# Cached keys doubled on load and turned inside the attention; counts, key splits, completions and row copies of a hybrid encoder step placed elsewhere

## The reference, cut to what matters

```python
# index scores, the top 256 keys of each query, then attention over these keys
logits = relu(einsum('bqhd,bld->bqhl', qi, ki))          # 8 indexer heads of 64
index  = einsum('bqhl,bqh->bql', logits, wi)
index  = where(admissible, index, -inf)                   # own chunk of 64 and all before
top_val, sel = top_k(index, 256)
s = einsum('bqkgd,bqnkd->bqkgn', qg, gather(k, sel)) * 64 ** -0.5   # 8 heads, 2 key heads
p = softmax(where(valid, s, -inf)); o = einsum('bqkgn,bqnkd->bqkgd', p, gather(v, sel))
```

## Time and profile before

| | us |
|---|---|
| median of 3 runs | 904.68 (904.44 to 906.88) |
| the profiled execution | 904.78 |
| its span | 903.2 |
| TensorE busy | 801.8 |
| VectorE busy | 484.6 |
| ScalarE busy | 335.1 |
| GpSimd busy | 166.5 |

### The profile page before, as it was taken

How to read it: one execution, slowest core, us unless ns; L and a number is a source line. 1 busy time by engine, 2 the same in 40 slices (tenths; PEclk the granted TensorE clock), 3 DMA queues, 4 the chain that set the end, 5 groups by cost and what they waited for, 6 DMA issues and landing times.

```text
span 903.2 us, 12302 instructions
## 1 busy us (share of the span) xinstructions
PE 801.8 (89%) x4185; PEld 673.1 (75%) x4185; DVE 484.6 (54%) x1188; ACT 335.1 (37%) x753; POOL 166.5 (18%) x361
## 2 busy tenths in 40 slices
PE   4788988898989999689489999999998999999984
PEld 3677877777877878578487788888886888888873
DVE  5523576778796877967852433333355433333323
ACT  4535545656566565566462111111125200000010
POOL 0323314040312103010103211111121111101101
PEclk9899969998989989979789999999999999999997
DMA  9322021211202002003425212111456443333331
GB/s 267 137 69 90 24 90 30 84 32 71 82 20 71 8 12 74 25 1 105 135 84 156 88 64 64 64 64 64 145 150 203 136 114 110 114 116 111 109 82 35
DMA packets 36206, 79.00 MB, mean 87 GB/s; under 512 B 7408, under 2 KB 9856, under 8 KB 34880
## 3 DMA queue, kind: packets, MB, share of 16 engines
q1 hardware_dynamic: 29712, 59.07, 21.0%
q0 software_dynamic: 6448, 19.36, 6.7%
HBM read 57.88 MB, written 20.53 MB: 87 GB/s over the span
## 4 chain that ended last, share of the span: by engine, by line
PE 60%; DVE 19%; issue 7%; ACT 6%; DMA 4%; POOL 2%; SPq 0%; DVEq 0%; POOLq 0%; ACTq 0%
PE bank L797 47%; DVE probs L1517 4%; DMA xT<-turned_x 3%; PE bank L912 3%; DVE work L1423 2%; DVE work L1458 1%; DVE top L1456 1%; PE bank L812 1%; PE bank L858 1%; PE bank L859 1%; PE bank L901 1%; DVE idx L1404 1%; PE bank L980 1%; PE bank L981 1%; PE bank L964 1%
## 5 line engine op out<-in xcount | busy, mean ns | idle before, releaser
L797 PE MATMUL bank<-w_hi,xT 128*128 128x512 f32 (+1 forms) x1152 | 378.8, 399 | 15.5 <-DVE xT L1343 6.7
L797 PEld LDWEIGHTS bank<-w_hi,xT 128*128 128x128 f32 x1152 | 221.0, 194 | 66.4 <-DMA xT<-turned_x 7.6
L797 PE MATMUL bank<-w_lo,xT 128*128 128x512 f32 (+1 forms) x576 | 226.9, 394 | 0.0
L797 PEld LDWEIGHTS bank<-w_lo,xT 128*128 128x128 f32 x576 | 112.2, 195 | 19.4
L912 PE MATMUL bank<-v_sb,pT 128*128 128x64 f32 x648 | 93.7, 286 | 11.3 <-ACT pT L1151 10.9
L912 PEld LDWEIGHTS bank<-v_sb,pT 128*128 128x128 f32 x648 | 87.1, 205 | 18.9 <-ACT pT L1151 18.1
L901 PE MATMUL bank<-ident,probs 128*128 128x128 f32 x324 | 56.8, 289 | 18.2 <-ACT probs L1140 18.0
L1404 DVE SCALAR_TENSOR_TENSOR idx<-bank,iw_s,idx 128x384 f32<-128x384 f32 (+5 forms) x93 | 53.7, 611 | 32.4 <-ACT bank L1186 31.5
L1140 ACT ACTIVATE probs<-probs,low 128x128 f32<-128x128 f32 (+8 forms) x68 | 54.7, 805 | 41.3 <-DVE low L1517 41.2
L1151 ACT COPY pT<-bank 128x512 f32<-128x512 f32 (+3 forms) x104 | 49.0, 495 | 42.5 <-PE bank L901 41.4
L901 PEld LDWEIGHTS bank<-ident,probs 128*128 128x128 f32 x324 | 40.9, 152 | 27.7 <-ACT probs L1140 25.6
(11 more groups left out here) (188 smaller groups left out, 1175.9 us busy)
## 6 DMA issues: line engine op xcount, KB each, us to landing
xT<-turned_x SPq DMA_DIRECT2D x34, 512.0 KB, 4.2
stage<-in_w_in SPq DMA_DIRECT2D x40, 256.0 KB, 3.2
turned_x<-xT SPq DMA_DIRECT2D x9, 1024.0 KB, 5.2
xin<-in_x_prompt SPq DMA_DIRECT2D x16, 256.0 KB, 3.9
early<-in_w_in SPq DMA_DIRECT2D x4, 1024.0 KB, 6.5
y_row<-in_x_prompt SPq DMA_DIRECT2D x16, 256.0 KB, 5.3
stage<-in_w_out SPq DMA_DIRECT2D x16, 256.0 KB, 3.2
out<-y_row POOLq DMA_DIRECT2D x16, 256.0 KB, 2.4
```

The lines of the kernel that those rows point to most:

```text
L797: mm = pe.matmul(out, (lo if which == 2 else hi)[:, k, :], (w_lo if which == 1 else w_hi)[slot][:, k, 0:width], start=(i == 0), stop=(i == ...
```

## The change

Six edits, all in the first part:

1. The cached rows are loaded doubled: two transfers write each 64-element piece side by side twice, so that one transpose fills both halves of the partitions, and one instruction of 128 partitions copies or splits a bank. The indexer keys take two staging buffers and two banks (ci 0 and 1), the keys two loads of xin and four banks (ck 0 for key head 0, ck 1 for key head 1, two banks each). Each has twice the transposes.
2. They are turned inside the attention: ci 0 and ci 1 behind heads 2 and 3 of attend(6), ck 0 behind head 5 of attend(7), ck 1 behind the first two heads' scores and the first exponential of attend(SAMPLE). SP's list has the second indexer load at tile 7, and the keys' loads ahead of and behind five blocks of rk.
3. The counts go with heads 2 to 6 in place of 1 to 5 (FIRST_COUNT); keep stays behind head 6.
4. "turn", the next tile's split, goes from behind head 5 to behind head 4 for all engines. That puts it ahead of head 7's scores.
5. The first completion comes when the list is done, the second behind the attended rows, then choose. Where the next tile is not searched (tiles 0 and 1) only choose moves.
6. ScalarE walks copy_order: its part of "iq", "kv" and "turn" comes two "turn" steps later than in the list.

GpSimd also waits for the sample tile's turned queries before it loads the last norm's gain. The diff, cut to its core:

```diff
+FIRST_COUNT = 2
...
-BETWEEN_HEADS = {1: "kv", 5: "turn"}
+BETWEEN_HEADS = {1: "kv", 4: "turn"}
...
+CACHED = {(NT - 2, 2): ("ci", 0), (NT - 2, 3): ("ci", 1), (NT - 1, 5): ("ck", 0)}
+
+
+def cached_banks(name, n):
+
+    return [("turn_ci", n)] if name == "ci" else [("turn_ck", n, half) for half in range(2)]
...
+    if t == SAMPLE:
+        order.append(("between", "ck", 1))
...
+        if (t, h) in CACHED:
+            order.append(("between", *CACHED[t, h]))
     return order + [("value", *last)]
+def copy_order(t):
+    order, held = [], []
+    for step in attention_order(t):
+        if step[0] == "between" and step[1] in ("iq", "kv", "turn"):
+            held.append([step, 2])
+            continue
+        order.append(step)
+        if step[0] == "turn":
+            for item in held:
+                item[1] -= 1
+            order += [item[0] for item in held if not item[1]]
+            held = [item for item in held if item[1]]
+    return order + [item[0] for item in held]
...
-                    sp.dma_start(buf[:].rearrange("p (b d) -> p b d", d=HD), ic).then_inc(done, 16)
+                    for to in range(2):
+                        sp.dma_start(buf[:].rearrange("p (b a d) -> p b a d", a=2, d=HD)[:, :, to, :],
+                                     ic[:, 4 * k:4 * k + 4, :]).then_inc(done, 16)
...
+            def load_cached_keys(g):
+
+                wait_filled(sp, ("turn_ck", 0, 1) if g else ("x1", "A", SAMPLE))
+                for to in range(2):
+                    sp.dma_start(xin[:].rearrange("p (b a d) -> p b a d", a=2, d=HD)[:, :, to, :],
+                                 kc[:, :, g * HD:(g + 1) * HD]).then_inc(ck_in, 16)
...
-                for i in {4: (27, 28), 5: (29, 30), 6: (31,), 7: (32,)}.get(t, ()):
+                for i in {4: (27, 28), 5: (29, 30), 6: (31,), 7: (32, 33)}.get(t, ()):
...
-            wait_filled(sp, ("x1", "A", SAMPLE))
-            sp.dma_start(xin[:].rearrange("p (b n) -> p b n", n=P), kc).then_inc(ck_in, 16)
-            for i in range(item_no["rk", STAGES], item_no["rg", 2 * STAGES]):
+            load_cached_keys(0)
+            for k in range(STAGES, KD):
+                load(item_no["rk", k])
+            load_cached_keys(1)
+            for i in range(item_no["rv", 0], item_no["rg", 2 * STAGES]):
...
+            def hi_cached_keys(g):
+                for half in range(2):
+                    key = ("turn_ck", g, half)
+                    wait_filled(act, key)
+                    ins = act.copy(kT_hi[:, g, half * BW:(half + 1) * BW], of(key)[:])
                 ins.then_inc(hi_ready, 1)
...
+            def lo_cached_keys(g):
+                dve.wait_ge(hi_ready, hi_no(f"ck{g}", "A", SAMPLE))
+                for half in range(2):
+                    c = slice(half * BW, (half + 1) * BW)
+                    key = ("turn_ck", g, half)
+                    dve.tensor_tensor(kT_lo[:, g, c], of(key)[:], kT_hi[:, g, c].bitcast(F32), ALU.subtract)\
+                       .then_inc(*drains(key))
...
-                        if 1 <= h <= COUNTS:
-                            search(t + 1, h - 1)
-                        if h == COUNTS + 1:
+                        if FIRST_COUNT <= h < FIRST_COUNT + COUNTS:
+                            search(t + 1, h - FIRST_COUNT)
+                        if h == FIRST_COUNT + COUNTS - 1:
                             keep(t + 1)
-                        if h == AH - 1:
-                            complete(t + 1, 0)
-                            complete(t + 1, 8)
-                if t != SAMPLE:
-                    wait_drained(dve, last_score(t, heads_of(t) - 1))
-                    choose(t + 1)
+                chosen = t != SAMPLE and searched(t + 1)
+                if chosen:
+                    complete(t + 1, 0)
                 heads = heads_of(t)
                 dve.wait_ge(exped, AH * t + heads)
                 dve.reciprocal(rden[:, 0:heads], den[:, 0:heads]).then_inc(ao_step, 1)
...
+                if chosen:
+                    complete(t + 1, 8)
+                if t != SAMPLE:
+                    wait_drained(dve, last_score(t, heads - 1))
+                    choose(t + 1)
...
+            wait_drained(pool, ("turn_aq", "A", SAMPLE))
```

More of the change, by code:

```diff
@@ L422, in take_attention @@
                     take_turned(step[2])
+                elif step[0] == "between" and step[1] in ("ci", "ck"):
+                    for key in cached_banks(*step[1:]):
+                        take(key)
                 elif step[0] == "between" and step[1] != "weights":
@@ L500, in hybrid_stream_step @@
         for t in range(TILES):
-            hi_order += [(s, t + 1) for s in ("x0", "x1", *hi_a) if t + 1 < TILES]
+            hi_order += [(s, t + 1) for s in ("x0", "x1") if t + 1 < TILES]
+            if t == NT - 1:
+                hi_order += [(f"ci{b}", t) for b in range(2)]
+            hi_order += [(s, t + 1) for s in hi_a if t + 1 < TILES]
+            if t == SAMPLE:
+                hi_order += [("ck0", t)]
             hi_order += [("turn_aq0", t), ("turn_aq1", t)]
-            if t == NT - 1:
-                hi_order += [("ci", t)]
             if t == SAMPLE:
-                hi_order += [(f"ck{b}", t) for b in range(2)]
+                hi_order += [("ck1", t)]
         hi_at = {(s, "A", t): i + 1 for i, (s, t) in enumerate(hi_order)}
@@ L593, in hybrid_stream_step @@
         items = (slot_items(0, "iq") + slot_items(1, "kv") + slot_items(2, "aq") + slot_items(3, "rq")
-                 + [(None, "ci", 0)]
+                 + [(None, "ci", b) for b in range(2)]
                  + slot_items(0, "rk") + slot_items(2, "rv") + slot_items(1, "rg")
@@ L613, in staged_at @@
             if i >= N_EARLY or i % EARLY == 0:
-                count[s.name] = count.get(s.name, 0) + 16 * (len(COLS[w]) if slot is not None else 1)
+                count[s.name] = count.get(s.name, 0) + 16 * (len(COLS[w]) if slot is not None else 2)
             return s, count[s.name]
@@ L646, in load @@
                     if slot2 is None:
[L647 removed]
+                        wait_filled(sp, ("turn_ci", k2))
                     else:
@@ L838, in index @@
                 if t == SAMPLE:
-                    wait_drained(pe, ("turn_ci", 0))
+                    for b in range(2):
+                        wait_drained(pe, ("turn_ci", b))
                 for kind, h, c in index_order(t):
@@ L881, in attend @@
                 if t == SAMPLE:
-                    for b in range(2):
-                        wait_drained(pe, ("turn_ck", b))
+                    wait_drained(pe, ("turn_ck", 0, 1))
                 for kind, h, n in attention_order(t):
@@ L892, in attend @@
                         a, b = chunks_of(t)[n]
+                        if t == SAMPLE and kv == 1:
+                            wait_drained(pe, ("turn_ck", 1, 1))
                         wait_free(pe, key)
@@ L1069, in hi_queries, with hi_cached_indexer @@
                     hi(key, packed(t, dst, a, half_rows(a)), turned_heads(t, key, a))
[L1071 to L1085 removed]
+            def hi_cached_indexer(b):
+                hi(("turn_ci", b), kiT_hi[:, b * BW:(b + 1) * BW])
+            def hi_cached_keys(g):
[3 more added lines that the diff above has]
+                    ins = act.copy(kT_hi[:, g, half * BW:(half + 1) * BW], of(key)[:])
                 ins.then_inc(hi_ready, 1)
@@ L1131, in between @@
                         round_w(w, k)
+                elif name == "ci":
+                    hi_cached_indexer(t)
+                elif name == "ck":
+                    hi_cached_keys(t)
             def attend(t):
-                for kind, h, g in attention_order(t):
+                for kind, h, g in copy_order(t):
                     if kind == "between":
@@ L1208, in _ @@
                     square_x(t + 2)
-                if t == NT - 1:
-                    hi_cached_indexer()
-                if t == SAMPLE:
-                    for half in range(2):
-                        hi_cached_keys(half)
                 if 2 <= t <= 5:
@@ L1562, in _ @@
                 lo_queries("turn_aq", t, aqT)
-                if t == NT - 1:
-                    lo_cached_indexer()
-                if t == SAMPLE:
-                    for half in range(2):
-                        lo_cached_keys(half)
                 if 2 <= t <= 5:
```

64 lines of the change are left out of this document (17 added, 47 removed).

## The result

The change is slower: 914.83 us (911.58 to 918.02, four runs) for 904.56 (902.77 to 906.88), ratio 1.0122, 95% interval 1.0085 to 1.0158. The forecast was slower too, but with 908.9 it has 4 us of the 10, and 914.83 lies above its range. The profiled execution took 914.52 us, its span is 913.0, 9.8 more than before.

A forecast was written before the change was run, and what follows sets the result against it. VectorE, not TensorE, was taken to set the end of the attention stages. Terms summed to +3.1 us, plus 1.0 for the clock: +4.1 on 904.78, so 908.9 us; range 898 to 914, the forecast's own 905.5 to 913.

The forecast's parts named there:

- Counts one head later: VectorE in attend(5): idle before head 4 grows from 0.87 to 2.1 us, and a 2.9 us count enters the gapless stretch.
- Rival A: Faster: VectorE has unseen slack, so the moved count costs nothing; 9.8 us gained, 895.0 us, chance 0.20.
- the waits of 1.56 and 0.26 us go: End of attend(5): TensorE no longer waits for VectorE's split of the next keys (1.56 us) or the output bank (0.26).
- where the clock fell at the boundary anyway nothing changes: Granted clock at attend ends: only attend(0) and attend(2) lose, 1.5 us, less 0.5 in the sample tile.
- the high bound of +4: Upper bound of the granted-clock term, booked at +1.0 us with bounds -2 and +4.
- cost zero: Second completion, choice and query split run during TensorE's 17 us index stage at no cost; 4.9 us without that cover.
- Attend(0): No counts there; the split ahead of head 7's scores waits for ScalarE: 2.5 us lost, bounds 1.5 and 3.5.
- ScalarE later: Later ScalarE copies free the copies of turned probabilities: 0.4 us before head 4 booked, upper bound 3 us.
- Gain 0.4 us, not 5.7: Cached indexer keys: the 5.74 us stall goes, but VectorE's first index addition in the sample tile comes only 0.4 us earlier.
- B: No change: half of each, gains in boundary waits and ScalarE's 3 us balance heads 7; 903 to 906 us, chance 0.25.
- Rival C: SP's queue: the store of turned x up to 2 us late, landing after 281; 911 us, chance 0.07 together with D.
- Rival D: Copy height is not free, so doubled copies and subtractions cost 3 us more in VectorE's stretch; 912 us, 0.07 with C.

The follow-up runs named there:

- cached and early split: On the kernel with only the cached keys doubled and turned inside the attention, the split moved ahead of head 7 in all tiles; 898.27 us, ratio 0.995.
- early split in 4 and 5: On the cached-keys-only kernel, split ahead of head 7, late ScalarE copies and completions behind the attended rows in attend(4) and attend(5) only; 889.74 us, ratio 0.9836.
- Cached alone: Kernel before the change with only the cached keys loaded doubled and turned inside the attention; 894.8 us, ratio 0.9928.
- The late completions alone: On the kernel with only the cached keys, completions and choice put behind the attended rows in attend(7) alone; 897.53 us, ratio 0.9922.

## Why the prediction was wrong

The sign was right, and so was the price of the moved counts. What failed is the step that took the waits at the end of each stage off the sum, and with it the clock behind the new gap. Forecast beside measured, us of difference; a stage runs from index start to index start, the last two are taken together up to the sample's first turn (452.11 before, 464.57 after).

| attend | 0 | 1 | 2 | 3 | 4 | 5 | 6 and 7 | rest |
|---|---|---|---|---|---|---|---|---|
| forecast | +2.5 | -0.4 | -0.5 | 0 | +1.4 | +0.6 | -0.5 | 0 |
| measured | +2.9 | -1.0 | +1.8 | +1.9 | +2.2 | +1.8 | +2.4 | -2.7 |

Measured adds up to 9.8 with 0.5 us before attend(0); the forecast's 3.1 had 1.0 for the clock on top.

*Counts one head later: right.* From a stage's start to head 7's last turn it is +2.2, -1.0, +1.0, +0.9, +2.5 and +2.2 us in attends 0 to 5; the recorded forecast has +2.5 for attend(0) and +2.4 for attend(5), and for attends 2 to 5 together its +1.5 with the 4.5 us of boundary waits added back, so 6.0; measured is 6.6. Rival A, in which VectorE has slack for the moved count, lies 13.9 us below the forecast (908.9 less 895.0), 1.0 of it for the clock; undoing the counts gave 13.1.

*The step that failed: "the waits of 1.56 and 0.26 us go".* That and its like in attends 2 to 4 took 4.5 us off the sum. From head 7's last turn to the next stage it is +0.8, +1.0, -0.3 and -0.4 instead, 5.6 us worse (some 1.3 us of the 4.5 lay behind the stage's first index matmul, so that this stretch misses them). The waits did go; the time went into the value matmuls and the turns of queries at a granted clock of 0.50. With the clock up and no wait the same four stretches took 2.27, 2.63, 2.19 and 2.19 us (attends 2 to 4 of cached and early split, attend(5) of early split in 4 and 5), in the change 3.86, 4.93, 3.46 and 3.59: 6.6 us for the lower clock. I had written that each attend now ends with a gap of about 3 us, and then "where the clock fell at the boundary anyway nothing changes". But the gap stands ahead of the values, not behind them, so more work runs slowly: 19 matmuls in 3.70 us at the end of attend(2), for 2.20 with the clock up. I booked 1.0 us for all of it (1.5 for attend(0) and attend(2), less 0.5 for the sample tile); the high bound of +4 would have covered about half of what was missed. The Trainium skill (TensorE: Matmul & The Clock Gate, What's actually happening) has the throttled state as the default that activity lifts; the trace agrees (0.50 behind the gaps of 3.79 and 3.91 us), and the sentence I drew from it, that the gap in every stage would cost, was the better forecast.

*The second completion, choice and query split "cost zero".* Their cover, an index stage of 17 us, is there for tiles 1 to 7 only. The sample's index stage is the short one: TensorE waits 2.93 us in it for tile 7's query split, and 7.22 us for the sample's query split. (Cached alone has 0.70 for tile 7's query split behind 2.23 for its key split, and 6.01, so these waits are not the completions' doing alone.) I added up VectorE's work in attend(7) and left out that completions had filled its waits for ScalarE and for head 7's values; moved behind them, they left 3.50 us idle there and 3.37 in attend(6). I put the 2.9 us missed in attends 6 and 7 down to this and to the lower clock at the end of attend(6) (4.24 us at 0.50, for 2.21 at 1.00 with cached and early split); how it divides was not tried. The late completions alone are shown by place (12.02 for 8.84 us), not in a total.

*Not in the forecast at all:* TensorE waits 2.26 and 2.06 us, in attends 4 and 5, for a bank that the early split still holds, ahead of head 6's last blocks:

```profile
266.37 0.45 PE L946 MATMUL bank<-ident,probs 128*128 128x128 f32 x1 [2.26 <-DVE w_lo L1384]
...
322.62 0.41 PE L946 MATMUL bank<-ident,probs 128*128 128x128 f32 x2 [2.06 <-DVE w_lo L1384]
```

In attend(6) the split of the cached indexer keys holds one for 2.04 us in the same way. With the counts at heads 1 to 5 and all else as in the change the first two are gone and the third is 0.66. This accounts for part of attends 4 and 5; how much was not tried separately.

*Attend(0):* +2.2 to its last turn against 2.5, and a clock of 0.52 behind a gap of 3.47 us. *ScalarE later:* booked at 0.4 us before head 4 alone; its price is 1.3 ± 4.6 us, unresolved. *The cached keys:* "Gain 0.4 us, not 5.7" was worked out for a kernel that has the counts late, and no run has the late counts without the cached keys; alone the part is worth 6.5 us. *Rival A, B:* out; A failed on its condition, a free count. *Rival C:* SP's store was indeed issued at 280.76 us in place of 229.31, and ScalarE's copy at 286.82 shows no wait for it; with a landing time of 5.2 us it had 0.9 us left. *Rival D:* two full-height subtractions of the cached keys took 1.28 us, so the doubling does what it says.

The rest is 2.7 us shorter, and TensorE's waits there for rows of the transfer xT<-turned_x are 3.2 us in all before (2.01 of it at 516 us) and 0.7 after. That this is the cause was not tested.

## What to carry to other kernels

Price a moved piece by the stretch it lands in: on top of the cached keys, a count moved by one head cost its whole length where VectorE had no gap from there to the end (attends 4 to 6), and 1.3 us at most in attends 1 to 3. When a wait is shifted from the end of a stage to ahead of its last matmuls, read the granted clock behind it, because the same wait then slows the work that follows. Before moving work that seems to stand in the way, look for the waits that it fills, and treat the last, shorter stages by themselves; here the good change was one part everywhere, and the early split with late completions in two tiles of nine.

## What the runs showed of the hardware

In the change, gaps of 3.79 and 3.91 us ahead of head 7's turn were followed by matmuls at a granted clock of 0.50 (attends 2 and 3). In cached and early split, gaps of 1.29, 1.28 and 0.49 us were followed by 0.98 to 1.00 (attends 2 to 4), but one of 1.12 us in attend(5) by 0.87 and then 0.50, with TensorE busy. In attend(5) of the change gaps of 1.11, 2.06 and 1.65 us were followed by 0.50 too, and in attend(3) with the split behind head 7 one of 1.55 us by 0.52. So no length of the last gap parts the two cases in these runs. 16 value matmuls of 64 columns took 3.52 and 1.99 us at the two levels.

The doubled loads of cached keys, 256 KB in pieces of 256 B, landed in 5.3 us (median of four), where 256 KB of weight rows took 2.8. Two of them are issued together, so part of that can be the neighbour. Before the change the one load of the cached indexer keys, also 256 KB in pieces of 256 B, took 4.2 us, where weight rows took 3.2; it had other transfers beside it (loads of x 1.2 us ahead, a store of x 1.1 us behind). The Trainium skill (DMA: Bandwidth & Descriptors, Specifications) wants 512 B for line rate, and the rows agree in direction; how much of the time is the size of the pieces no run here shows.

```profile
stage<-in_w_in SPq DMA_DIRECT2D x40, 256.0 KB, 2.8
xin<-in_cache_k SPq DMA_DIRECT2D x4, 256.0 KB, 5.3
```

Before the change:

```profile
stage<-in_w_in SPq DMA_DIRECT2D x40, 256.0 KB, 3.2
stage<-in_cache_kidx SPq DMA_DIRECT2D x1, 256.0 KB, 4.2
```
